# An upper bound on the row index of the indirect transfers in the expert blocks of a hybrid diffusion step

## What is computed

```python
def moe(x2d, router_w, router_bias, exp_w1, exp_w3, exp_w2, shared_w1, shared_w3, shared_w2):
    ...
    _, eidx = lax.top_k(jnp.where(emask, sb, -jnp.inf), TOP_K)          # TOP_K = 8
    ...
    padded = (counts + MOE_BLOCK - 1) // MOE_BLOCK * MOE_BLOCK          # MOE_BLOCK = 128
    ...
    def expert_block(args):
        tok, e = args
        xb = x2d[tok]
        hb = jax.nn.silu(xb @ exp_w1[e]) * (xb @ exp_w3[e])
        return hb @ exp_w2[e]

    yb = lax.map(expert_block, (slot_tok.reshape(NB, MOE_BLOCK), block_expert))
    routed = jax.ops.segment_sum(yb.reshape(P, D) * slot_w[:, None].astype(x2d.dtype), slot_tok, num_segments=N)
    shared = (jax.nn.silu(x2d @ shared_w1) * (x2d @ shared_w3)) @ shared_w2
    return routed + shared
```

## Time and profile before

| | |
|---|---|
| median of 3 runs | 2313.21 us (2312.15 to 2313.41) |
| profiled execution | 2313.95 us, its span 2312.2 us |
| busy share of the span | PE 86%, PEld 57%, DVE 55%, ACT 43%, POOL 30% |
| DMA | 422.47 MB; q1 (issued by SP) 30.1%, q0 (issued by POOL) 27.2% of 16 engines' time |
| expert stage, first weight load to last scatter's landing | about 983 to 2259 us |

### The profile page before, as it was taken

How to read it: one execution, slowest core, us unless ns; L and a number is a source line. 1 busy time by engine, 2 the same in 40 slices (tenths; PEclk the granted TensorE clock), 3 DMA queues, 4 the chain that set the end, 5 groups by cost and what they waited for, 6 DMA issues and landing times. The chain is left out here.

```text
span 2312.2 us, 31162 instructions
## 1 busy us (share of the span) xinstructions
PE 1992.8 (86%) x8459; PEld 1320.8 (57%) x8460; DVE 1268.4 (55%) x2023; ACT 1005.5 (43%) x1445; POOL 704.4 (30%) x643
## 2 busy tenths in 40 slices
PE   6697998999798798179999999999999999999970
PEld 1343444578687354157676666676666666666740
DVE  2566554002877589555565555665655555565646
ACT  1344542101223111056565556666555565555641
POOL 4111000000000124513435545434444445455440
PEclk9699999999999899579999999999999999999985
DMA  9243201100000632089689988777888989897465
GB/s 300 99 160 115 69 18 46 37 19 19 10 1 26 251 121 83 20 326 344 180 268 310 302 282 284 217 193 220 248 267 274 340 273 311 306 290 201 107 177 195
DMA packets 110114, 422.47 MB, mean 183 GB/s; under 512 B 19300, under 2 KB 33636, under 8 KB 85100
## 3 DMA queue, kind: packets, MB, share of 16 engines
q1 hardware_dynamic: 62508, 261.05, 30.1%
q0 software_dynamic: 47248, 160.70, 27.2%
q10 hardware_dynamic: 304, 0.02, 0.0%
HBM read 336.61 MB, written 85.66 MB: 183 GB/s over the span
## 5 line engine op out<-in xcount | busy, mean ns | idle before, releaser
L1775 DVE TENSOR_TENSOR wupl<-w,wuph 128x2048 fp32r<-128x2048 f32 x232 | 521.3, 2288 | 547.3 <-ACT wuph L1741 547.3
L1741 ACT ACTIVATE wuph<-w 128x2048 fp32r x232 | 432.2, 1918 | 36.6 <-SPq L1565 33.9
L1692 PE MATMUL bank<-w,hT 128*128 x912 | 416.2, 599 | 0.3
L1674 PE MATMUL bank<-wuph,xTh 128*128 128x512 f32 x920 | 369.7, 402 | 20.1 <-DVE xTl L1784 19.9
L1674 PE MATMUL bank<-wuph,xTl 128*128 128x512 f32 x920 | 361.3, 393 | 0.0
L1674 PE MATMUL bank<-wupl,xTh 128*128 128x512 f32 x920 | 360.7, 392 | 0.0
L1692 PEld LDWEIGHTS bank<-w,hT 128*128 128x128 f32 x912 | 165.6, 192 | 170.8 <-issue 170.8
L1626 POOL DMA_INDIRECT xg<-hn_scratch,idx_g x118 | 212.6, 1802 | 95.5 <-POOL idx_g L1618 91.8
L1731 ACT ACTIVATE y<-bank 128x512 f32<-128x512 f32 x114 | 68.1, 598 | 360.9 <-POOLq L1631 203.0
L1634 POOL DMA_INDIRECT yacc_scratch<-y,idx_s x114 | 188.5, 1654 | 115.1 <-ACT y L1732 64.2
L1674 PEld LDWEIGHTS bank<-wuph,xTh 128*128 128x128 f32 x920 | 174.3, 189 | 58.5 <-issue 24.8
(11 more groups left out here) (314 smaller groups left out, 2248.9 us busy)
## 6 DMA issues: line engine op xcount, KB each, us to landing
w<-in_exp_w SPq DMA_DIRECT2D x192, 1024.0 KB, 8.9
wada<-in_w_ada POOLq DMA_DIRECT2D x16, 1024.0 KB, 6.7
wg<-in_w_in SPq DMA_DIRECT2D x12, 1024.0 KB, 5.7
wada<-in_w_ada SPq DMA_DIRECT2D x4, 2048.0 KB, 15.5
yacc_scratch<-zero POOLq DMA_DIRECT2D x10, 512.0 KB, 8.4
x<-x_scratch SPq DMA_DIRECT2D x9, 512.0 KB, 4.1
x_scratch<-x SPq DMA_DIRECT2D x9, 512.0 KB, 2.6
hn_scratch<-hn SPq DMA_DIRECT2D x9, 512.0 KB, 2.9
```

The source lines that it names most:

```text
L1674: mm = pe.matmul(b_up[j][:, :], x[:, k, :], w[:, :, k, :], start=(k == 0 and i == 0), stop=(k == KT - 1 and i == 2))
L1692: mm = pe.matmul(b_down[half][:, :], hT[:, i, :], w2[:, bass.ds(slot, 1), i, half * 512:(half + 1) * 512].rearrange("p s n -> p (s n)"), s ...
L1741: act.activation(part13(wup[j][0], half), raw13(e % WSLOT, half), ACT.Copy).then_inc(w_high, 1)
L1775: dve.tensor_tensor(part13(wup[j][1], half), raw13(e % WSLOT, half), part13(wup[j][0], half).bitcast(F32), ALU.subtract).then_inc(w_low, 1)
```

## The change

Both indirect transfers get an upper bound N - 1 = 1151 for the row index, and an index above it is not an error. A pad's index is 1152 or more, so its row is neither gathered nor scattered. A row of `xg` whose slot is a pad keeps what it held before; so that this is a number in the first blocks, POOL clears both buffers once, ahead of the first gather, and waits for it. Later such rows hold rows of earlier blocks, and their weight of 0 makes the hidden row 0.

```diff
@@ stage_experts, gpsimd
-                pool.indirect_dma_start(xg[j][:, :], None, m.hn2, bass.IndirectOffsetOnAxis(ap=idx_g[j][:, :], axis=0)).then_inc(gathered[j], 16)
+                pool.indirect_dma_start(xg[j][:, :], None, m.hn2, bass.IndirectOffsetOnAxis(ap=idx_g[j][:, :], axis=0),
+                                        bounds_check=N - 1, oob_is_err=False).then_inc(gathered[j], 16)
...
                 pool.indirect_dma_start(m.yacc, bass.IndirectOffsetOnAxis(ap=idx_s[:, :], axis=0), y[j][:, :], None,
-                                        compute_op=ALU.add).then_inc(scattered, 16)
+                                        compute_op=ALU.add, bounds_check=N - 1, oob_is_err=False).then_inc(scattered, 16)
...
             n = pairs(pool)
             pool.sem_inc(scatter_done, 2)
+            for j in range(2):
+                pool.memset(xg[j][:, :], 0.0).then_inc(pool_step, 1)
+            pool.wait_ge(pool_step, 2)
             gather(0, 0, True)
```

## The result

The changed kernel takes 2299.28 us, the median of seven runs (2293.85 to 2306.73); the kernel before took 2313.41 in seven runs beside them (2312.15 to 2321.46). The ratio is 0.9927, with a 95% interval of 0.9911 to 0.9943: faster by 0.7%, where 1.6% were forecast. In us that is 14 by the two medians and 17 by the ratio. The direction and the range hold, the size does not. The cause turned out to be another one than the prediction's, and a version that removes it takes 2248, where the kernel before took 2320 beside it.

What follows compares the result with a forecast made beforehand. Stalls from late gathered rows, put down to DMA load, were taken to bound the kernel beside TensorE's work. 2312.2 - 38 + 2.1 - 1 = 2275.3, with 1.0 between span and median 2276 us; range 2236 to 2309.

Steps and rivals of the forecast that it cites:

- What bounds the kernel: Expert stage: TensorE's own work is 1135.7 of 1218.1 us; 82.4 are stalls, from gathered rows coming late.
- The difference is DMA load: Expert stage: scatters lie 10.5 us apart in stalled stretches, 8.6 in quiet ones, because DMA engines are 0.93 against 0.72 busy.
- The load per block: Expert stage: a block that is its expert's only one asks for 12.2 us of DMA in 10.05.
- Fewer rows: Gathers and scatters in the expert stage: skipping pads gains between 75 us and nothing; 38 us taken as the middle.
- backlog sum: Expert blocks: DMA demand carried on, less 10.05 us per block; excess over a 2.3 us slack is stall; 5 us left.
- The estimate by the Trainium skill's dealing: Indirect moves: if engines serve two runs of four partitions, some 52 us of stalls stay, for a time near 2286.
- The check: Bound on POOL's indirect moves: taken as costing nothing, 1.4 us of slack covering it; bounds -1.6 to +3.2 per scatter.
- POOL becomes the bound: Rival: comparing indices lengthens a scatter's issue from 1.6 to 4.8 us, 11.8 per block, time 2428; chance 0.11.
- Two memsets and a wait: Start of the expert stage: clearing both xg buffers ahead of the first gather costs +2.1 us, bounds 0.5 and 4.
- The tail: End of the kernel: the last scatter's wait shortens with a lighter all-pad gather, -1 us, bounds -3 and 0.
- Packets of q0 fall by 0.3: Sign on POOL's queue: packets fall by about 0.3 of what blocks move, else the change doesn't do what it says.
- If the share falls and the intervals stay, the busiest engine is the limit: Sign in single-block stretches: DMA share falls from 0.93 but intervals stay at 11 to 14 us.

Runs made afterwards that it cites:

- Experiment 8: Kernel before, with odd blocks adding into a second array, so a scatter waits for the last but one; second array never read; 2234.26 us, ratio 0.9636.
- spread rows: Changed kernel with the token of rank r in slot 7r mod 128 of its block, so valid rows lie over all partitions; 2280.85 us, ratio 0.9831.
- two sums: Odd blocks add into a second array, so scatter b waits for b-2 alone; on the kernel before 2234.26 us, 2248.23 with both arrays added at the end.

## Why the prediction was right or wrong

**What bounds the kernel: right up to the last step.** That 82.4 us are stalls, that weights are not their cause, that `xg` is late because of POOL's order of scatters and gathers: all of this stands. The step that failed is "The difference is DMA load" and the paragraph "The load per block" built on it. A share of busy time was read as work that has to fit: 12.2 us of demand in 10.05. Experiment 8 moves the same rows and weights through the same ten blocks with a share of 1.00 and no stall. These blocks took 107 us of all engines' time before (0.93 of 115) and 100 there: the time of packets is no fixed amount of work that can be added up block by block. The Trainium skill warns of this in Perfetto Trace Analysis, "Identifying the Most-Contended Engine": with 16 DMA engines occupancy misleads. The trace agrees, 1.00 beside no stall and 0.83 beside one stall after another; what the page puts in its place, the bytes moved, doesn't name the line either, with 306 GB/s in the stalled stretch and 346 in the one without a stall. What had to fit into 10.05 us was one step of the line, from a scatter to the next. The prediction had that period in hand, 8.6 us in a quiet stretch and 10.5 in a stalled one, and took it for an effect of the load only. In the kernel before, over the 56 steps longer than 10.2 us, it is 11.55 us from a scatter's start to the copy of the next index, and 1.29 from there to the next scatter: 12.84.

What stays open is why a landing takes that long. Without the order a landing has two blocks' time instead of one, and so experiment 8 shows that the engines can carry all the bytes in TensorE's time, and that one block's time for a landing is what was short. It does not show that a landing is independent of the load.

**Fewer rows, -38: measured -22.4, and that net of the check.** The two ends (75 and nothing) came from the backlog sum, so the middle between them had no ground. What the bound really shortens is a landing. These are means of the time from a scatter's start to the copy of the next index, worked out from POOL's timeline for blocks behind which POOL waited 0.95 us or more (in brackets how many), by the real rows that the reference's routing gives the block:

| real rows | before | change | change, spread rows |
|---|---|---|---|
| up to 40 | 10.58 (15) | 9.66 (13) | 8.96 (15) |
| 41 to 90 | 9.57 (22) | 9.15 (22) | 8.05 (24) |
| 91 to 127 | 9.96 (9) | 10.17 (9) | 9.26 (10) |
| 128 | 9.85 (47) | 9.70 (47) | 10.07 (46) |

Leaving out two thirds of a scatter's rows and more saves 0.9 us of 10.6. Blocks behind which POOL no longer waits drop out of a mean; over all 20 blocks with up to 40 rows it is 9.72 before and 8.61 in the change. Block 28, with 24 real rows, shows it: in the kernel before its scatter starts at 1330.53 and the next index is copied at 1342.95, 12.42 later; in the changed kernel

```profile
1334.62 1.59 POOL L1635 DMA_INDIRECT yacc_scratch<-y,idx_s  x1 [1.04 <-issue]
...
1345.53 0.18 POOL L1618 COPY idx_s<-shared 128x1 int32 x1 [7.20 <-issue]
```

10.91 for 24 rows. The rest is not the rows'. In the shared expert's stretch, with no weights beside it, a full scatter landed in 6.1 us; I read the remainder as the wait behind the weights in each engine, which no run isolates. Spreading the rows helps the small scatters further (8.96, 8.05) and the full ones not at all, so **the dealing matters, as the prediction supposed, but within the line**: 60.0 to 49.1 us of stalls.

The estimate by the Trainium skill's dealing (DMA: Bandwidth & Descriptors, "The descriptor swizzle"), 52 us of stalls kept and 2286 us, lay nearer to the measured 60.0 and 2299 than the middle did. It rests on the same backlog sum, so this speaks for the order of size only.

**The check, at nothing: wrong.** The slack of 1.4 us that should cover it was read in a quiet stretch, but the stalls are where the line has none. There the whole 0.06 us counts, and the measured 8 us (3 to 13) would be about a third of what the skip brought (14 to 17 net, so 22 to 25 without them). The price itself lay within the bounds given (-1.6 to +3.2 a scatter). The rival "POOL becomes the bound" named the right mechanism, a longer scatter line, and gave it a size fifty times too large.

**Two memsets and a wait, +2.1: right.** 1.84 us of clearing, first gather 2.0 later behind the first weight load, block 0 2.1 later.

**The tail, -1: not seen.** 84.2 and 84.8 us. It moved where the prediction did not look: with the rows spread or with two sums the last scatter starts 13.2 us after the last hidden transposes instead of 21.4 (before) or 22.4 (change), and the end is 78.5 to 80 where the final stage is the same. I read that as the line having no lag left to work off.

**The signs.** "Packets of q0 fall by 0.3": they don't fall at all, and still the change does what it says; the bytes were the sign. "If the share falls and the intervals stay, the busiest engine is the limit": the share fell to 0.83 and they stayed, but the limit was a wait. ScalarE's wait on POOL fell from 203.0 to 152.6, by a quarter as the stalls did.

## What to carry to other kernels

When a transfer waits for the landing of the one before, ask first for the period of that line in the stretch that stalls, and only then for bytes: taking away 36.65 MB gave 14 to 17 us; taking away the order between neighbours gave some 72 us with every byte still moved and the second array added up, and 84 without that last step. A cost that a slack is to cover has to be compared with the slack of the stalled stretch, not of the quiet one. And the longest waits of an engine off the bound are worth a second look where the bounding engine's waits lead back to it: 449 us in 93 blocks stood in the list of waits from the beginning.

## What the runs showed of the hardware that I had not expected

- A row that the bound skips stays in the queue as a packet under 512 B: 8960 rows skipped, 8960 small packets more, the sum of q0's packets unchanged at 47248.
- The bound lengthens an indirect move's way to issue by some 0.06 us on POOL (gather 1.00 to 1.05 or 1.06 in its short form, copy of the index to scatter 1.10 to 1.16), rows skipped or not.
- A busy share of 1.00 of all 16 DMA engines over 100 us, at 346 GB/s, stood beside a TensorE that never idled. The share of 0.93 in the stalled kernel was no sign of its bound.
- POOL's gather has two lengths, 1.00 us and about 2.25 (70 of 118 are over 1.2 in the kernel before), and its copy of an index takes 0.18 us or up to 2.8. The trace shows what they meet: all 70 long gathers overlap VectorE's making of the weights' low part (`wupl`, line 1775), and so do all 19 long copies of a scatter's index. In the kernel before:

```profile
1526.17 4.49 DVE L1775 TENSOR_TENSOR wupl<-w,wuph 128x2048 fp32r<-128x2048 f32 x2 [3.96 <-ACT wuph L1741]
...
1528.78 1.93 POOL L1618 COPY idx_s<-shared 128x1 int32 x1 [3.54 <-DMA yacc_scratch<-y,idx_s]
```

The copy ends at 1530.71, 0.05 us after VectorE's two operations. In experiment 8 no gather and no copy of a scatter's index overlaps that work, and all have the short form. These copies are not what stalls the kernel before: the 19 are 26 us longer than the short form, but only three of them, with 4.8 us, lie in steps of the line longer than 10.2 us. The gathers lie beside a scatter's flight; what their long form costs was not tried.
